# Letting VectorE sum a part of the gathered expert rows in two of six blocks, with the mix finished earlier beside them

## The reference

```python
a = jnp.einsum('tkd,td->tk', u_tab[e_blk], x_blk).astype(jnp.float32)
w = (g_blk * jax.nn.gelu(a, approximate=False)).astype(x_blk.dtype)
return jnp.einsum('tk,tkd->td', w, v_tab[e_blk])
```

## Time and profile before

| | us |
|---|---|
| median of 3 runs (2513.31 to 2525.56) | 2515.28 |
| the profiled execution | 2519.05 |
| its span, first to last instruction | 2517.1 |
| PE busy (85%) | 2144.1 |
| DVE busy (58%) | 1448.1 |
| ACT busy (33%) | 839.5 |
| POOL busy (35%) | 875.8 |
| moved by DMA, mean 382 GB/s | 962.00 MB |

### The profile page before, as it was taken

One profiled execution on the slowest core, in us unless ns is written; L12 is line 12 of the kernel. 1 busy time (PEld: TensorE's weight loads), 2 busy tenths in 40 slices (PEclk: granted clock), 3 DMA queues, 4 the chain that ended last, 5 costly groups with the idle time before them and its releaser, 6 DMA issues.

```text
span 2517.1 us, 22186 instructions
## 1 busy us (share of the span) xinstructions
PE 2144.1 (85%) x7370; PEld 1168.9 (46%) x7370; DVE 1448.1 (58%) x3171; ACT 839.5 (33%) x2632; POOL 875.8 (35%) x772
## 2 busy tenths in 40 slices
PE   7997999999787788798888899989978877877775
PEld 5675655666233344354443565556523333332222
DVE  0156466456898545545758355644786676544454
ACT  2423376232223223533223346532222222322222
POOL 0001245223345444343434234422244444443431
PEclk8997999999899899899898899999989998999998
DMA  9958999899799999999999799988879999999995
GB/s 397 420 208 357 359 365 413 318 394 376 321 415 421 422 421 422 397 415 420 420 421 421 280 356 374 419 322 335 351 304 421 422 421 419 407 422 422 421 422 247
DMA packets 142626, 962.00 MB, mean 382 GB/s; under 512 B 15920, under 2 KB 24240, under 8 KB 28208
## 3 DMA queue, kind: packets, MB, share of 16 engines
q0 software_dynamic: 110592, 805.36, 78.3%
q1 hardware_dynamic: 30912, 152.06, 15.4%
q10 hardware_dynamic: 1008, 3.17, 0.3%
HBM read 958.17 MB, written 2.36 MB: 382 GB/s over the span
## 4 chain that ended last, share of the span: by engine, by line
PE 50%; DMA 27%; DVE 16%; ACT 3%; issue 2%; SPq 0%; POOL 0%; DVEq 0%; POOLq 0%; ACTq 0%
PE acc L700 28%; DMA uv_rows<-in_peer_uv,experts 26%; PE pair L756 8%; PE pair L815 6%; DVE uv_rows L1203 6%; PE pair L641 1%; PE pair L720 1%; PE pair L793 1%; PE pair L619 1%; DMA uv_rows<-in_w_mod 1%; PE pair L609 1%; DVE arena L1131 1%; DVE arena L1166 1%; DVE arena L1168 1%; DVE picked L1169 1%
## 5 line engine op out<-in xcount | busy, mean ns | idle before, releaser
L700 PE MATMUL acc<-uv_rows,diag 128*128 128x512 f32 x3072 | 1462.1, 628 | 244.8 <-ACT diag L892 244.8
L588 POOL DMA_INDIRECT uv_rows<-in_peer_uv,experts x768 | 875.6, 1140 | 1599.4 <-PE acc L700 1286.1
L1203 DVE CUSTOM_DVE_ANT_0 uv_rows<-uv_rows,h_tok 128x1024 f32<-128x1024 f32 x768 | 920.1, 1224 | 561.8 <-DMA uv_rows<-in_peer_uv,experts 558.0
L700 PEld LDWEIGHTS acc<-uv_rows,diag 128*128 128x128 f32 x3072 | 598.7, 201 | 1046.5 <-issue 668.6
L884 ACT ACTIVATE gelu<-dots 128x2 f32<-128x2 f32 x384 | 78.1, 203 | 1089.2 <-DVE dots L1203 1088.8
L892 ACT ACTIVATE diag<-consts,weight 128x128 f32<-128x128 f32 x768 | 260.3, 386 | 0.0
L756 PE MATMUL pair<-wtiles,hT 128*128 128x256 f32 x912 | 206.4, 385 | 12.4 <-ACT hT L848 12.4
L756 PEld LDWEIGHTS pair<-wtiles,hT 128*128 128x128 f32 x912 | 176.1, 193 | 49.9 <-issue 26.7
L834 ACT COPY arena<-pair 128x256 f32<-128x256 f32 (+3 forms) x154 | 84.6, 552 | 318.3 <-PE pair L815 133.3
L888 ACT ACTIVATE weight<-gelu,gates 128x1 f32<-128x1 f32 x768 | 184.3, 287 | 12.6
L815 PE MATMUL pair<-hT,wtiles 128*128 128x256 f32 (+1 forms) x768 | 143.0, 344 | 0.0
(11 more groups left out here) (113 smaller groups left out, 1259.5 us busy)
## 6 DMA issues: line engine op xcount, KB each, us to landing
uv_rows<-in_w_mod SPq DMA_DIRECT2D x32, 1024.0 KB, 20.1
wtiles<-in_peer_wq SPq DMA_DIRECT2D x24, 1024.0 KB, 9.1
wtiles<-in_w_in SPq DMA_DIRECT2D x23, 1024.0 KB, 9.3
wtiles<-in_w_mod SPq DMA_DIRECT2D x16, 1024.0 KB, 13.2
uv_rows<-in_peer_uv,experts POOLq DMA_INDIRECT x768, 14.4
wtiles<-in_w_out SPq DMA_DIRECT2D x12, 1024.0 KB, 7.1
uv_rows<-in_peer_wq SPq DMA_DIRECT2D x8, 1024.0 KB, 8.1
rows<-in_ln_g SPq DMA_DIRECT2D x12, 512.0 KB, 10.8
```

The costliest lines, as they stand in the source:

```text
L588: pool.indirect_dma_start(out=uv_rows[:, slot, :, :].rearrange("p t d -> p (t d)"), out_offset=None, in_=i["peer_uv"], in_offset=bass.Indi ...
L700: last = nc.tensor.matmul(acc[:, half, :], diag[:, slot, :], uv_rows[:, slot, 1, half * 512:(half + 1) * 512], start=False, stop=True, ski ...
L1203: nc.vector.tensor_tensor_reduce(out=uv_rows[:, slot, 0, :], in0=uv_rows[:, slot, 0, :], in1=h_tok[:, slot_q, :], scale=1.0, scalar=0.0, o ...
```

## The change

In blocks 0 and 3, of the rows k < 96, those with n % 3 = 2 (32 rows per block) are no longer summed by PE. DVE adds them to `dve_sum` in SBUF, one turn after their dot products, ahead of the dot products of that turn, and waits for ACT's weights for it. ACT makes no diagonal for them. At the end of such a block DVE adds `dve_sum` to `acc`. POOL waits for `row_added` instead of `row_used` where the old row of a place was one of DVE's. The diagonals have 6 places of their own, and ACT waits until the row that used one is done. The clearing matmuls go: the first row of a block overwrites `acc`. Beside blocks 0 and 3 five turns instead of two stay after the last step of the mix.

```diff
+DIAGS = 6
...
-    s += beside(0, mix_start(1) + mix_middle(1) + mix_end(1) + query_steps(1), 2)
+    s += beside(0, mix_start(1) + mix_middle(1) + mix_end(1) + query_steps(1), 5)
...
-    s += beside(3, mix_start(3) + mix_middle(3) + mix_end(3) + query_steps(3), 2)
+    s += beside(3, mix_start(3) + mix_middle(3) + mix_end(3) + query_steps(3), 5)
...
+SHARED_WITH_DVE = (0, 3)
+def summed_by_dve(n):
+    return n // PER_TOKEN in SHARED_WITH_DVE and n % 3 == 2 and n % PER_TOKEN < 96
+def summed_before(n):
+    by_dve = sum(summed_by_dve(k) for k in range(n))
+    return n - by_dve, by_dve
...
-                        pool.wait_ge(row_used, n - RING + 1)
+                        by_pe, by_dve = summed_before(n - RING + 1)
+                        if summed_by_dve(n - RING):
+                            pool.wait_ge(row_added, by_dve)
+                        else:
+                            pool.wait_ge(row_used, by_pe)
...
-                    for n in range(2):
-                        nc.tensor.matmul(acc[:, n, :], const("zero")[0:1, :], consts[0:1, 0:512], start=True, stop=True)
...
+                        if summed_by_dve(n):
+                            continue
+                        pe.wait_ge(diag_ready, summed_before(n + 1)[0])
                         for half in range(2):
-                            last = nc.tensor.matmul(acc[:, half, :], diag[:, slot, :],
+                            last = nc.tensor.matmul(acc[:, half, :], diag[:, summed_before(n)[0] % DIAGS, :],
                                                     uv_rows[:, slot, 1, half * 512:(half + 1) * 512],
-                                                    start=False, stop=True, skip_group_check=True)
+                                                    start=(n % PER_TOKEN == 0), stop=True, skip_group_check=True)
...
                     for j in range(G):
+                        if summed_by_dve(first + j):
+                            continue
                         act.wait_ge(weight_ready, first + j + 1)
+                        before = summed_before(first + j)[0]
+                        if before >= DIAGS:
+                            act.wait_ge(row_used, before - DIAGS + 1)
...
+                        if q in SHARED_WITH_DVE:
+                            dve.wait_ge(row_added, summed_before(PER_TOKEN * (q + 1))[1])
+                            nc.vector.tensor_tensor(zz, acc[:, :, :], dve_sum[:, :].rearrange("p (a n) -> p a n", a=2),
+                                                    ALU.add).then_inc(acc_drained, 1)
+                            dve.wait_ge(acc_drained, q + 1)
+                            link(nc.vector.tensor_tensor(zz, zz, gate_b, ALU.mult))
...
+                def add_rows(h):
+                    for n in range(q * PER_TOKEN + h * G, q * PER_TOKEN + (h + 1) * G):
+                        if not summed_by_dve(n):
+                            continue
+                        slot, before = n % RING, summed_before(n)[1]
+                        dve.wait_ge(weight_ready, n + 1)
+                        if before:
+                            dve.wait_ge(row_added, before)
+                        if before == summed_before(q * PER_TOKEN)[1]:
+                            nc.vector.tensor_scalar(dve_sum[:, :], uv_rows[:, slot, 1, :], weight[:, slot:slot + 1], None,
+                                                    ALU.mult).then_inc(row_added, 1)
+                        else:
+                            nc.vector.scalar_tensor_tensor(out=dve_sum[:, :], in0=uv_rows[:, slot, 1, :],
+                                                           scalar=weight[:, slot:slot + 1], in1=dve_sum[:, :],
+                                                           op0=ALU.mult, op1=ALU.add).then_inc(row_added, 1)
+
+                for h in range(h0, h1):
+                    if 1 <= h <= GROUPS:
+                        add_rows(h - 1)
+                    for j in range(G if h < GROUPS else 0):
```

More of the change, by code:

```diff
@@ L338 @@
 for _name, _n in (("ident", P), ("ones", P), ("rope", 2 * 2 * HD), ("dft_ctx", 2 * P), ("dft_lat", 2 * 2 * 2 * P),
-                  ("dft_ch", 2 * P), ("window", GRID_W), ("halves", 2), ("iota", TOPK), ("zero", P)):
+                  ("dft_ch", 2 * P), ("window", GRID_W), ("halves", 2), ("iota", TOPK)):
     CONST[_name] = (_at, _at + _n)
@@ L402, in hybrid_step @@
         weight = sb("weight", [P, RING])
-        diag = sb("diag", [P, RING, P])
+        diag = sb("diag", [P, DIAGS, P])
+        dve_sum = sb("dve_sum", [P, D])
         qkv = arena[:, 0:2 * IN_W].rearrange("p (b n) -> p b n", b=2)
@@ L469, in hybrid_step @@
         row_used = sem("row_used")
+        row_added = sem("row_added")
         gelu_ready = sem("gelu_ready")
@@ L697, in experts_sum @@
                         slot = n % RING
-                        pe.wait_ge(diag_ready, n + 1)
+                        if summed_by_dve(n):
+                            continue
+                        pe.wait_ge(diag_ready, summed_before(n + 1)[0])
                         for half in range(2):
-                            last = nc.tensor.matmul(acc[:, half, :], diag[:, slot, :],
+                            last = nc.tensor.matmul(acc[:, half, :], diag[:, summed_before(n)[0] % DIAGS, :],
                                                     uv_rows[:, slot, 1, half * 512:(half + 1) * 512],
-                                                    start=False, stop=True, skip_group_check=True)
+                                                    start=(n % PER_TOKEN == 0), stop=True, skip_group_check=True)
                         last.then_inc(row_used, 1)
@@ L890, in expert_weights @@
                     for j in range(G):
+                        if summed_by_dve(first + j):
+                            continue
                         act.wait_ge(weight_ready, first + j + 1)
-                        nc.scalar.activation(diag[:, slot + j, :], ident, ACT.Copy,
+                        before = summed_before(first + j)[0]
+                        if before >= DIAGS:
+                            act.wait_ge(row_used, before - DIAGS + 1)
+                        nc.scalar.activation(diag[:, before % DIAGS, :], ident, ACT.Copy,
                                              scale=weight[:, slot + j:slot + j + 1]).then_inc(diag_ready, 1)
@@ L1066, in layer_norm @@
                     else:
-                        dve.wait_ge(row_used, PER_TOKEN * (q + 1))
-                        nc.vector.tensor_tensor(zz, acc[:, :, :], gate_b, ALU.mult).then_inc(acc_drained, 1)
-                        dve.wait_ge(acc_drained, q + 1)
+                        dve.wait_ge(row_used, summed_before(PER_TOKEN * (q + 1))[0])
+                        if q in SHARED_WITH_DVE:
[5 more added lines that the diff above has]
+                        else:
+                            nc.vector.tensor_tensor(zz, acc[:, :, :], gate_b, ALU.mult).then_inc(acc_drained, 1)
+                            dve.wait_ge(acc_drained, q + 1)
                     link(nc.vector.scalar_tensor_tensor(out=z, in0=x, scalar=ALPHA, in1=z, op0=ALU.mult, op1=ALU.add))
@@ L1196, in expert_dots @@
                     wait_drained(dve, ("H2", q))
-                for h in range(h0, min(h1, GROUPS)):
-                    for j in range(G):
+                def add_rows(h):
[9 more added lines that the diff above has]
+                                                    ALU.mult).then_inc(row_added, 1)
+                        else:
+                            nc.vector.scalar_tensor_tensor(out=dve_sum[:, :], in0=uv_rows[:, slot, 1, :],
[5 more added lines that the diff above has]
+                    for j in range(G if h < GROUPS else 0):
                         n = q * PER_TOKEN + h * G + j
```

## The result

The changed kernel takes 2481.96 us in the median of four runs (2481.05 to 2483.55), the kernel before 2520.42 in four (the forecast was worked from 2515.28, the median of the first three of these). The ratio is 0.986 with a 95% interval of 0.9835 to 0.9884: 1.4% faster. The forecast was 2466 in a range of 2428 to 2505, so direction and range held, and the saving was forecast about a third too large: 49 us against 36.6 us between the two profiled spans (2517.1 and 2480.5).

The account below looks back on a forecast made before the run. PE, or PE beside DMA's floor of 5.0 us per turn, was taken to bound block 0. Block 0 -23, block 3 -25 and small edits -1 sum to -49 us: 2519 to 2470, median near 2466, range 2428 to 2505.

Parts of the forecast that it names:

- the queries: Stage up to `top` 2, PE saturated: fewer rows and one turn less, -12 us in block 0, -10.6 in block 3.
- block 0's projection: Input projection of block 0, nine turns before and after: PE sums four rows fewer, -7 us.
- The output projection: Stage after the attention: fewer rows on PE, -7 us in block 0; with one turn less, -10.5 in block 3.
- The attention: Block 0 goes from PE's 128 us to DMA's 120, taken as 122: -6 us; block 3: 0.
- rival A: DVE's turn sets the attention, +8 us instead of -6, norms +10; median 2508 us, chance 0.14.
- The restart: From the list of experts to the next block's first row: its place comes free late, +5 us per block.
- From `top` 2 to the list: DVE busy with the same steps, no additions: 0 in block 0; one turn less in block 3, -2.3 us.
- the norms: Layer norms, where DVE is the bound: four additions join its queue, +4 us per block, 0 to +10.
- The turns: Three turns per block move from before `pick` 5 to behind it, taking 10.6 us of PE work off block 0's list.
- B: Rival of the full saving: only DMA is left in the way, -57 us per block, median 2401; chance 0.12.
- C: Rival: PE starves behind the new wait, projections and queries lose their gain, +23 us per block, median 2561; chance 0.07.
- D: Rival: each of 64 additions lengthens a POOL issue by 1.04 us, +67 us, median 2533; chance 0.07.

Follow-up runs that it names:

- the run with two turns: The changed kernel with DVE adding its rows two turns after their dot products instead of one, everything computed: 2469.67 us, -12.3 against the changed kernel.
- the small edits: The changed kernel with no row given to DVE and two turns, not five, behind the mix: 2511.09 us, against 2520.42 for the kernel before.

## Why the prediction was right, and where it was off

**The bound and the relief.** Right. PE's group lost 1462.1 - 1349.1 = 113 us, as said. Where PE was the bound and DVE idle, in the queries and in block 0's projection, the rows' 1.77 us came back in full: -13.7 and -12.1 against -12 and -10.6, and -8.7 against -7. Block 3's projection looks as good, -11.1 against -10.5, but by two errors that cancel: I had counted 6 rows fewer there, and PE sums 20 instead of 28, worth 14 us. DVE waits for ACT's weights for 20.9 us in this stage.

**The output projection is the step that failed.** I subtracted rows from PE's time: -7 and -10.5, measured -0.5 and -1.4. DVE still waits there for PE's end, 12.25 and 12.02 us instead of 16.14 and 15.29, so PE's part was the path, as said. But it holds waits beside its rows, and I had put these at nothing: once PE is no longer the late engine, it meets a handover that its lateness had hidden. In block 0 PE sums 7 rows in the stretch instead of 12 (-8.9 us). It waits 5.3 us longer at the gate, and then needs 1.8 us more for the four matmuls and 1.1 for the first tile: -0.7 in all. In block 3 it sums 6 rows instead of 10 (-7.1), waits 3.8 us longer and needs 1.5 us more: -1.8 in all. The turn that I took out of block 3's stretch for -3.5 is replaced by one that stood in the attention. The run with the gate moved confirms it with 4.5 us in block 0.

**The attention.** -6 and 0 against -4.3 and -3.4 looks right, but this is luck, since the reason was not. I had DMA's pace end the stage, 24 x 5.0 = 120 us at 415 to 420 GB/s; the trace has 120.1 us in block 0 at 377 GB/s. Seven additions wait for ACT there, as many as forecast, 10.8 us together. I had added such waits to DVE's own time and found the sum below the floor. They were on the path: with the wait gone or hidden the stage is 8 to 11 us shorter. DMA's pace does bound it, but lower: in the run with two turns 44 dot products fall between the two marks of block 0, not the 48 of 24 turns. That is 110 us at 2.5 us each, the stage takes 109.9, and DMA moves 406 GB/s in it at a share of 1.00. So rival A, DVE's turn, was half true, not at its price of +8. Its sign, steps over 10.5 us, was no test: from one `neg_max` to the next block 0 has steps of 12.5, 13.5 and 15.0 us, but the kernel before has up to 11.5 there and 13.3 in block 3.

**The restart.** +5 forecast, +7.5 and +7.8 measured: 1.7 us for the row at the lower clock, and 0.8 us from its end to POOL's issue.

**From `top` 2 to the list, and the norms.** 0 and -2.3 forecast, +2.8 and 0 measured. DVE is as busy there as forecast, 50.0 and 50.1 us before and after in block 0, 50.1 and 47.9 in block 3. But it is not busy throughout: ahead of the last `top` it waits for ACT's copy of the scores, in block 0 for 2.73 us, where it had no such wait, and in block 3 for 4.21 instead of 2.75. In the norms +4 stands against +3.9 and -0.8; what block 3 gained there no run shows.

**The turns.** In the sum they stand for -6, -3.5 and +5 in block 0 and -3.5, -3.5, -2.3 and +5 in block 3, -9 us together. With sharing beside them they gave -6.4, a little more than the spread, alone nothing (2251.7 against 2250.8). POOL's two waits for the list of 22 and 25 us did vanish, and 8 us of restart each came in their place.

**The other rivals.** B fell with the handovers. C fell: PE's idle time at diagonals rose from 244.8 to 280.9 us in the whole span, but projection and queries kept their gain. D fell: POOL's mean issue went from 1140 to 1164 ns, and DMA stood at 409 GB/s in the queries where it had 379.

**The signs.** POOL's two waits are gone and PE's group lost what was said. But block 1's first row is issued 15.1 us earlier, not 20 to 26, and block 4's 35.5, not 45 to 52; and DVE's wait for ACT's weights is 97 us (9.3 of it at the first row of a block), not 20 to 50. This wait is the sign that pointed at the error in the attention.

## What to carry to other kernels

In this kernel, work taken from the engine that is the bound was worth its full price only in stages without handovers between engines. After such a change, look for waits of the relieved engine that its lateness had covered, and move the other side's instruction ahead of whatever it now waits for. A wait at the head of an engine's turn should be far enough behind the producer to find its result ready: the edit that adds rows one turn later than the change does was worth a third as much again as the whole change. A floor from a rate has to be counted with the rows that really fall between the two marks, and the DMA share in the stage says whether it is what holds the stage.

## What the runs showed that was not expected

The start of the program, which no edit touched, ended between 217.2 and 233.5 us in the profiles. In the longest one the granted clock in the first 100 us was 0.80 and DMA moved 269 GB/s from 100 to 216 us; in the profiles of the changed kernel and of the small edits it was 0.95, with 306 GB/s. Medians of kernels that differ by 5 us are hard to tell apart through this. The time between the first and the last row leaves the start out, but has some 5 us of its own; for edits of blocks 0 and 3 the sum of these two blocks is the better measure.
